# The first column parts of three stages split by token tile, and the later query rests moved from GpSimd to VectorE

## The reference: what is computed

```python
q = (rmsnorm(x) @ w_q).reshape(T, 8, 2, 128)              # queries, w_q is 1024 x 2048
s = einsum('thpc,hpkc->thpk', q, sub_keys)                # scores against 2 x 128 keys
top_s, top_i = top_k(s, 16)                               # picks in each half
fin_s, fin_pos = top_k(top_s[0][:, None] + top_s[1], 16)  # 16 experts of 16384 per head
act = gelu(einsum('thkd,td->thk', expert_u[idx], h))
out = einsum('thk,thkd->td', softmax(fin_s) * act, expert_v[idx])
```

## Time and profile before

| | us |
|---|---|
| median of 3 runs | 2014.12 (2011.47 to 2016.54) |
| the profiled execution, its own time | 2012.58 |
| span of its instructions | 2010.8 |
| PE busy | 1658.6 (82%) |
| DVE, ACT, POOL busy | 988.1, 547.6, 616.4 |
| DMA, mean | 316 GB/s |

### The profile page before, as it was taken

How to read it: one execution, slowest core, us unless ns; L and a number is a source line. 1 busy time by engine, 2 the same in 40 slices (tenths; PEclk the granted TensorE clock), 3 DMA queues, 4 the chain that set the end, 5 groups by cost and what they waited for, 6 DMA issues and landing times.

```text
span 2010.8 us, 21920 instructions
## 1 busy us (share of the span) xinstructions
PE 1658.6 (82%) x8644; PEld 1020.0 (51%) x8644; DVE 988.1 (49%) x1894; ACT 547.6 (27%) x951; POOL 616.4 (31%) x396
## 2 busy tenths in 40 slices
PE   7998977677777777777999998999999867676765
PEld 7784942232222223236999988987884311111211
DVE  6462666876778775553663886554434100000001
ACT  4342421212222212123453544445622000000001
POOL 3431643444444444433674105443320000000000
PEclk9999998999999999998999999999999877778878
DMA  8755499999999999984544433554586999999997
GB/s 336 302 200 217 191 374 421 422 420 421 421 421 421 418 419 414 419 366 149 171 165 159 147 106 126 187 186 156 184 348 248 422 421 422 421 421 421 421 422 319
DMA packets 92228, 634.73 MB, mean 316 GB/s; under 512 B 10940, under 2 KB 13628, under 8 KB 16472
## 3 DMA queue, kind: packets, MB, share of 16 engines
q1 hardware_dynamic: 50832, 353.39, 45.1%
q0 software_dynamic: 36864, 268.45, 32.4%
q10 hardware_dynamic: 4424, 11.42, 1.6%
HBM read 632.15 MB, written 1.08 MB: 315 GB/s over the span
## 4 chain that ended last, share of the span: by engine, by line
PE 47%; DMA 42%; DVE 7%; ACT 2%; issue 2%; POOL 0%; SPq 0%; DVEq 0%; ACTq 0%
DMA t<-in_expert_uv,t 21%; PE ps L555 6%; PE ps L557 6%; PE ps L560 6%; DMA t<-in_eg 6%; DMA ring<-in_ed 5%; DMA t<-in_ed 5%; PE ps L596 3%; PE ps L755 3%; DMA ring<-in_eg 3%; PE ps L609 3%; PE ps L758 3%; DVE t L2018 3%; PE ps L575 2%; PE ps L576 2%; PE ps L581 2%
## 5 line engine op out<-in xcount | busy, mean ns | idle before, releaser
L179 POOL TENSOR_TENSOR t<-ring,t 128x1024 fp32r<-128x1024 f32 x125 | 320.8, 2576 | 474.7 <-ACT t L171 474.4
L755 PE MATMUL ps<-t 128*128 128x512 f32 x496 | 275.6, 638 | 163.3 <-ACT t L1384 163.2
L2685 POOL DMA_INDIRECT t<-in_expert_uv,t x248 | 280.9, 1133 | 360.3 <-PE ps L758 340.1
L2018 DVE CUSTOM_DVE_ANT_0 t<-t 128x1024 f32<-128x1024 f32 x248 | 303.0, 1226 | 171.9 <-DMA t<-in_expert_uv,t 169.4
L171 ACT ACTIVATE t<-ring 128x1024 fp32r<-128x1024 f32 x220 | 230.6, 1054 | 238.8 <-PE ps L560 87.2
L758 PE MATMUL ps<-t 128*128 128x512 f32 x496 | 260.0, 606 | 0.0
L755 PEld LDWEIGHTS ps<-t 128*128 128x128 f32 x496 | 87.3, 195 | 326.1 <-ACT t L1384 261.8
L1057 PE MATMUL ps<-t 128*32 128x512 f32 x864 | 144.5, 765 | 74.6 <-DMA t<-in_eg 28.0
L179 DVE TENSOR_TENSOR t<-ring,t 128x1024 fp32r<-128x1024 f32 x95 | 129.2, 1366 | 134.9 <-ACT t L171 132.1
L555 PE MATMUL ps<-t 128*128 128x256 f32 x1120 | 164.7, 291 | 15.1 <-ACT t L171 5.5
L1377 ACT ACTIVATE t<-t 128x2 f32<-128x2 f32 x129 | 26.2, 203 | 507.9 <-DVE t L2018 507.5
(11 more groups left out here) (358 smaller groups left out, 1841.5 us busy)
## 6 DMA issues: line engine op xcount, KB each, us to landing
ring<-in_w_in SPq DMA_DIRECT2D x82, 1024.0 KB, 5.0
t<-in_eu SPq DMA_DIRECT2D x38, 1024.0 KB, 26.9
t<-in_eg SPq DMA_DIRECT2D x36, 1024.0 KB, 26.9
t<-in_ed SPq DMA_DIRECT2D x34, 1024.0 KB, 27.3
ring<-in_ed SPq DMA_DIRECT2D x30, 1024.0 KB, 27.0
ring<-in_eg SPq DMA_DIRECT2D x28, 1024.0 KB, 26.8
ring<-in_eu SPq DMA_DIRECT2D x26, 1024.0 KB, 27.1
ring<-in_ada_w SPq DMA_DIRECT2D x20, 1024.0 KB, 7.5
```

Of the source, the lines that this page charges most:

```text
L179: e.tensor_tensor(p.lo, p.view, p.hi.bitcast(F32), ALU.subtract).then_inc(self.w.lo[eng], 1)
L755: ins = e.matmul(sums[tt][0], s.diag[col % 4], v[:, 1024:1536], start=first, stop=last)
L2018: ins = e.tensor_tensor_reduce(out=g[:, 0:1024], in0=g[:, 0:1024], in1=s.hN[:, col // 128, :], scale=1.0, scalar=0.0, op0=ALU.mult, op1=AL ...
L2685: m.gathered[s.place[col]].up(e.indirect_dma_start(out=s.gb[col], out_offset=None, in_=m.a_in["expert_uv"], in_offset=bass.IndirectOffsetO ...
```

## The change

1. Part 0 of the first stage, parts 0 to 2 of the queries and parts 0 to 3 of `iq` are each done in two halves of 24 matmuls on 128 token columns. The first halves (`pe_cols_begun`) are put ahead of the work on tile 1: in the first stage after the transposes of both tiles and before the wait for tile 1's rest, in the two others before the transposes of tile 1. The second halves stand where the whole parts stood.
2. The rests of the query parts 7 to 15 are all made by DVE. Before, 10, 12 and 14 were. Parts 7 and 8 are made inside the picks of head 0 (after 10 and after 17 steps), 9 and 10 behind them, 15 behind the second weighting. POOL makes none between the gathers.
3. The rests of all four `iq` parts are made by DVE before `finish(1)`; before, two were.
4. The banks that hold the begun sums of `iq` are put last in the order in which banks are claimed.

```diff
-        s.sp.expect(pair(a["w_q"], n), ("G", "G", "GGVG", "VGVG")[n], "cols")
+        s.sp.expect(pair(a["w_q"], n), ("G", "GGGV", "V", "V")[n], "cols")
...
+def pe_part(e, sp, p, o, xs, cols):
+    xh, xl = xs
+    for k in range(8):
+        e.matmul(o, p.hi[:, k, :], xh[:, k, cols], start=k == 0, stop=False)
+    for k in range(8):
+        e.matmul(o, p.hi[:, k, :], xl[:, k, cols], start=False, stop=False)
+    sp.rest(e, p)
+    for k in range(8):
+        ins = e.matmul(o, p.lo[:, k, :], xh[:, k, cols], start=False, stop=k == 7)
+    return ins
+
+def pe_cols_begun(m, e, sp, key, xs, n):
+    begun = []
+    for i in range(n):
+        if i % 2 == 0:
+            ps = m.b.claim(e, sub(key, i // 2))
+        p = sp.take(e, "pe")
+        pe_part(e, sp, p, ps[:, i % 2 * 256:i % 2 * 256 + 128], xs, slice(0, 128))
+        begun.append((ps, p))
+    return begun
...
+            if i < len(begun):
+                ps, p = begun[i]
+                ins = pe_part(e, sp, p, ps[:, j * 256 + 128:j * 256 + 256], xs, slice(128, 256))
...
     e.wait_ge(*b.taken(("hT1", 0, 1)))
+    begun = pe_cols_begun(m, e, s.sp, "p", s.hT, 1)
     e.wait_ge(*b.taken(("hT1", 1, 1)))
...
+    e.wait_ge(*b.taken(("hT2", 0, 1)))
+    begun = pe_cols_begun(m, e, s.sp, ("q", 0), s.hT, 3)
     pe_turn_tile(m, e, "hT2", s.hN[:, 1, :], 1, m.normed)
-    e.wait_ge(*b.taken(("hT2", 0, 1)))
     e.wait_ge(*b.taken(("hT2", 1, 1)))
...
-    b.usable = list(range(8))
+    e.wait_ge(*b.taken(("hT3", 0, 1)))
+    m.begun = pe_cols_begun(m, e, m.s3.sp, ("iq", 0), m.s3.hT, 4)
+    held = [b.at["iq", 0, n][0] for n in range(2)]
+    b.usable, b.next = [i for i in range(8) if i not in held] + held, 0
...
-    run(dve_picks(m, e, 0, 0, (0,)))
+    picks = dve_picks(m, e, 0, 0, (0,))
+    pour(picks, 10)
+    s.sp.lows(e, "V", s.q0 + 8)
+    pour(picks, 7)
+    s.sp.lows(e, "V", s.q0 + 9)
+    run(picks)
...
     weighted(1)
+    s.sp.lows(e, "V", s.q0 + 16)
...
-    m.s3.sp.lows(e, "V", 2)
+    m.s3.sp.lows(e, "V", 4)
     run(finish(1))
...
-    s.sp.lows(e, "G", s.q0 + 10)
+    s.sp.lows(e, "G", s.q0 + 7)
     for col in range(256):
-        if col in (3, 6, 7):
-            s.sp.lows(e, "G", s.q0 + 12 + 2 * (3, 6, 7).index(col))
```

More of the change, by code:

```diff
@@ L543, in pe_turn_tile, with pe_cols @@
         m.b.told(ins, (key, tt, kq))
-def pe_cols(m, e, sp, key, xs):
+def pe_part(e, sp, p, o, xs, cols):
     xh, xl = xs
+    for k in range(8):
[15 more added lines that the diff above has]
+    return begun
+def pe_cols(m, e, sp, key, xs, begun=()):
     for half in range(2):
-        ps = m.b.claim(e, sub(key, half))
+        if 2 * half >= len(begun):
+            ps = m.b.claim(e, sub(key, half))
         for j in range(2):
[L552 to L560, removed]
+            i = 2 * half + j
+            if i < len(begun):
+                ps, p = begun[i]
+                ins = pe_part(e, sp, p, ps[:, j * 256 + 128:j * 256 + 256], xs, slice(128, 256))
+            else:
+                p = sp.take(e, "pe")
+                ins = pe_part(e, sp, p, ps[:, j * 256:j * 256 + 256], xs, slice(0, 256))
             sp.through[p.n] = m.b.told(ins, sub(key, half))
@@ L676, in pe_mixers1 @@
     e.wait_ge(*b.taken(("hT1", 0, 1)))
+    begun = pe_cols_begun(m, e, s.sp, "p", s.hT, 1)
     e.wait_ge(*b.taken(("hT1", 1, 1)))
     for key in "pcbv":
-        for j, _ in enumerate(pe_cols(m, e, s.sp, key, s.hT)):
+        for j, _ in enumerate(pe_cols(m, e, s.sp, key, s.hT, begun if key == "p" else ())):
             pour(ada, 2 - j % 2)
@@ L763, in pe_retrieval @@
     for n in range(4):
-        for part, _ in enumerate(pe_cols(m, e, s.sp, ("q", n), s.hT)):
+        for part, _ in enumerate(pe_cols(m, e, s.sp, ("q", n), s.hT, begun if n == 0 else ())):
             p = 4 * n + part
@@ L792, in pe_attention @@
     pe_turn_tile(m, e, "hT3", r3(m.hold, 2)[:, 1, :], 1, m.finished)
-    e.wait_ge(*b.taken(("hT3", 0, 1)))
     e.wait_ge(*b.taken(("hT3", 1, 1)))
-    run(pe_cols(m, e, s.sp, ("iq", 0), s.hT))
+    run(pe_cols(m, e, s.sp, ("iq", 0), s.hT, m.begun))
     run(pe_cols(m, e, s.sp, ("aq", 0), s.hT))
```

## The result

The changed kernel takes 2034.91 us, the median of 5 runs (2027.36 to 2039.78), and the kernel before 2014.62 beside it, the median of 5 (2011.47 to 2016.54): a ratio of 1.0094 [1.0075, 1.0114]. (The ratios here are taken over all the runs, so they differ a little from the ratio of two medians.) It is slower by 20 us. The forecast was 2012.6, its range ended at 2019, and slower had a chance of 0.15. The profiled execution has a span of 2033.1 us against 2010.8, and its mean granted clock of TensorE is 0.931 against 0.939. The five times of the changed kernel spread over 12 us, those of before over 5, and only one execution of each has a trace. So 22.3 us are to be found.

The account below looks back on a forecast made before the run. The chain was taken as PE for 47% and DMA for 42%, PE setting the stage beginnings. Terms -0.2 (first stage), +0.3 (second), 0 (rests), -1.6 (third) sum to -1.5 us: 2012.6 against the median 2014.12; range 1999 to 2019.

Parts of the forecast that it names:

- The pace: Half parts: a 128-column matmul costs 0.111 us, bounds 0.108 to 0.120, so a half takes 2.66 us against 2.88 whole.
- The cheap: Rival for the half parts: 128-column matmuls cost 0.067 to 0.081 us; with 0.067 together -14 us, 2000; chance 0.15.
- the dear rival: Half parts: 128-column fp32r matmuls run as two records like plain fp32, 0.22 us; together +42 us, 2056; chance 0.09.
- the clock: Stage beginnings: slow spell gone in the second stage, PE pausing only 1.57 us; in the first, clock up by 18.9.
- The list at the end: Signs of a wrong prediction: pace outside 0.108 to 0.120, clock falling in pauses, PE waiting between 228 and 262 us.
- The second: Second stage: the second halves of the query parts end at 212.69 against 212.37 before, +0.3 us.
- The third: Third stage: the second halves of `iq` end at 934.82 against 936.42 before, -1.6 us.
- The first: First stage: part 1 ends at 24.5 against 24.74, -0.2 us; +1.1 or -1.5 by when the clock rises.
- The range's lower end of -4.2: Whole kernel: the sum's best case, with the pace bounds and those of the first stage giving -4.2 to +2.8 us.
- The late transposes: Tile 1's transposes queue behind the begun halves, ending at 203.13 and 922.60; ACT's later work and the keys stay covered.
- The rests: Queries and picks: rests on DVE stall PE nowhere, 0 on the path; first gather near 227.6, gathers 6, 7 later.
- One for one: Gather stream: column 12 waits for PE's last scores, so their shift moves the stream and all behind it equally.

Follow-up runs that it names:

- experiment 7: The kernel before, with groups of useless fp32r matmuls of several shapes in PE's idle stretches of the second and third stage; one execution, 2015.34 us.
- Experiment 1: The changed kernel with no part begun early and the bank order as before, so only the rests are moved; 2014.37 us, ratio 0.9995 to the kernel before.
- experiment 5: The changed kernel with only the first stage's part begun early, rests still moved; 2015.86 us, ratio 1.0003 to the kernel before.
- Experiment 2: The changed kernel, but the second time each begun part runs whole, on all 256 columns; 2020.85 us, ratio 1.0024 to the kernel before.
- Experiment 3: The changed kernel with eight useless 512-column matmuls behind the late transposes in the second and third stage; 2018.82 us, ratio 1.0010 to the kernel before.
- Experiment 6: The kernel before, with useless 128-column matmuls (32 and 12, 65 and 24) in PE's idle stretches of the second and third stage; 2010.33 us, ratio 0.9978.

## Why the prediction was wrong

**The pace was right.** Eight half matmuls took 0.89 us, 0.111 to 0.112 each, at the high clock. The begun halves took 7.99 and 10.67 us for 8.0 and 10.66, and experiment 7 shows the cause that was argued from L904 and L739, the weights. The cheap and the dear rival both fell.

**The step that failed is the clock.** The prediction said of the second stage: "In this the slow clock is already gone: PE pauses only 1.57 us in place of 4.0 and then 1.6." It took 8 us of work without a pause ahead of the transposes for enough. PE's pause came out at 1.75 us, and soon behind it, at 208.9 and again at 935.9, the granted clock fell, for 17.1 and 23.9 us; before it had been low for 6.8 and 10.2. In the first stage, "With PE busy from 11.82 without a pause I let it rise by 18.9" failed alike: the clock rose at 28.0. (Before it rose at 22.2, not at the end of the part at 21.3 as the prediction read it.) The list at the end did name "if the clock falls in the 1.6 us pauses (some +2.5 in each stage)". The event was named and its size was wrong by a factor of three to five (8.3 and 11.6 us with the scores and the parts behind), because the recovery was taken from before, where whole parts ran in the slow spell and ended it.

**What the runs showed in its place.** At the low clock, the halves did not bring the high one back: not in 12 us of unbroken work in the second stage (208.9 to 221.3), not in 20 in the third (935.9 to 956.2), not in some 10 from 13.79 on in the first. It came 2.8 to 3.8 us into the whole parts of 256 columns each time. Where these two stages begin with whole parts (before, experiments 1 and 5) the low stretches were 6.8 to 13.7 us long, began ahead of the first part and ended 3.3 to 5.6 us into it. Experiment 2 shows it from the other side: with 256 columns in the second parts the fall stays away or lasts 3.4 us. Experiment 3 shows that with the pause filled both products run at 1.00 and the stage terms come out within 0.7 us of the forecast. Experiment 6 shows that short matmuls can hold the clock when only gaps of 0.6 us and less interrupt them, and 7 that they may not hold it always. So with this shape the clock is hard to regain, which three places show; that it is also easier to lose rests on one stage of experiment 2 and one fall in 7, and is not settled. By what rule the chip decides is not shown, and whether the weight loads or the columns count for it is open, since no run held one of them fixed at the low clock for long enough.

The Trainium skill, same page, section "HAM oscillation — how this bites in real kernels", tells of short groups of matmuls with waits between them that fall back to the slow clock again and again. The two falls behind the pauses look like it, but the waits there are of some 3 to 5 us and the pauses here of 1.75. What it makes the cause, PE's idle gaps, does not account for the 18 us at 0.50 with PE busy for all of them, nor for the fall at 913.5 in experiment 7.

**Term by term.** The second stage was to give +0.3 and gave +8.8: 6.1 in the second halves, 0.9 in the first scores, 1.3 in the first whole part, 0.2 in the longer pause. The third was to give -1.6 and gave +10.4: 9.9, 1.7 and 0.2 above it in the same terms, and 0.2 because the prediction counted PE's free moment by the start of a matmul (911.07) and the end of the product by a later measure (936.42; by starts 936.26), so that its own gain was rather -1.4. The first was to give -0.2, or +1.1 with the clock rising where it did before; it gave +4.1 at PE, since the clock rose later than in either case, and 2.3 at its end. The range's lower end of -4.2 is also more than its terms give: -0.1, -2.2 and -1.5 are -3.8. Neither slip decides anything beside the clock.

**The late transposes** were as forecast but for the shift of the first stage: 8.0 and 10.7 us behind PE's free moment, in front of the pause. By standing behind the begun halves they put the pause between the two halves, and nothing else is seen to be late by them.

**The rests** were right at nothing. Experiment 1 shows the picks 2.6 us shorter (2.5 was forecast) and, counted from the first scores, gathers 6 and 7 later by 1.8 and 3.4 (1 and 3). PE waited for no rest between 228 and 262 us in it. In the changed kernel the first gather is at 238.64, 17.4 us behind the first scores: the picks stood behind parts that the slow PE had not reached, and that cost nothing either, as column 12 goes out 1.16 us behind the last scores in both.

**One for one.** That a shift of PE's last scores is a shift of the whole gather stream was right: 11.11 us at the scores, 11.07 at PE's last column.

## What to carry to other kernels

Eight matmuls of 128 columns with full weights took 0.89 us and eight of 256 columns 0.96, so work begun early on half of the columns costs nearly its whole price again later: read the price of the load before that of the columns. Before short matmuls are put at a stage's beginning, ask at which clock they will run and what will raise it: here they stayed at half speed for 18 us and more, where whole parts at a stage's beginning were at full speed again 3.3 to 6.1 us after their start. At the low clock halves cost as much as whole ones. If PE idles in front of a critical product, useless matmuls in the gap (also behind the transposes, while another engine splits) gave 4 us here, more than the begun halves did in any run.

## What was not expected of the hardware

The granted clock stood at 0.50 for 18.00 us in which PE was busy for 18.00 (937 to 955 us), and fell once from 1.00 with PE at work (913.5 us in experiment 7). After the same pause of 1.75 us it fell in one stage and not in the other, in the same execution (experiment 2: not at 204.7, but at 926.8), so one execution does not tell whether such a pause is safe. With 32 columns of weights in place of 128, an fp32r matmul of 128 columns came every 0.061 us instead of 0.111.
